# A mixture-of-experts block on one core: one table load before the expert loop, the second half's transposes one unit earlier, relu and silu back to back

## The reference

```python
def expert_block(args):
    xb, e = args
    gu = xb @ w_gate_up[e] + b_gate_up[e]
    gate = jnp.minimum(gu[:, :D_FF], SWIGLU_LIMIT)
    up = jnp.clip(gu[:, D_FF:], -SWIGLU_LIMIT, SWIGLU_LIMIT)
    act = (up + 1.0) * (gate * jax.nn.sigmoid(SWIGLU_ALPHA * gate))
    return act @ w_down[e] + b_down[e]
```

## Time and profile before

| | us |
|---|---|
| median of 3 runs | 2231.53 (2229.44 to 2234.69) |
| profiled execution, its own time | 2228.01 |
| its span, first to last instruction | 2226.2 |
| PE busy | 2065.4 (93%) |
| expert loop, first `turn_rows` to last `down` | 741 to 2185 |

### The profile page before, as it was taken

One profiled execution on the slowest core, in us unless ns is written; L12 is line 12 of the kernel. 1 busy time (PEld: TensorE's weight loads), 2 busy tenths in 40 slices (PEclk: granted clock), 3 DMA queues, 4 the chain that ended last, 5 costly groups with the idle time before them and its releaser, 6 DMA issues.

```text
span 2226.2 us, 37885 instructions
## 1 busy us (share of the span) xinstructions
PE 2065.4 (93%) x11367; PEld 1602.5 (72%) x11368; DVE 1540.9 (69%) x1941; ACT 1467.8 (66%) x1944; POOL 397.0 (18%) x519
## 2 busy tenths in 40 slices
PE   6889999899886599999999999999999999999997
PEld 4678778777675478787787777777776777676683
DVE  4466565544456678889798687886785787675595
ACT  4466676643331478888787686786785787675583
POOL 2222212011234111111121121111110111011022
PEclk9899999869797799999999999999999999999996
DMA  5301010211115699999799898998996899796694
GB/s 177 62 21 29 20 29 20 76 48 57 40 59 182 235 308 371 379 369 378 274 363 326 285 337 287 320 371 276 312 377 225 296 343 314 276 315 242 219 318 177
DMA packets 250411, 507.21 MB, mean 228 GB/s; under 512 B 44454, under 2 KB 62676, under 8 KB 250228
## 3 DMA queue, kind: packets, MB, share of 16 engines
q1 hardware_dynamic: 234724, 462.98, 59.0%
q0 software_dynamic: 15632, 43.53, 7.6%
HBM read 470.25 MB, written 38.54 MB: 229 GB/s over the span
## 4 chain that ended last, share of the span: by engine, by line
PE 68%; DVE 12%; issue 10%; ACT 5%; DMA 4%; POOL 1%; DVEq 0%; SPq 0%; ACTq 0%; POOLq 0%
PE bank L1038 23%; PE bank L1060 12%; PE bank L1072 6%; PE bank L809 6%; DVE w_low L1858 6%; PE bank L908 4%; PE bank L1089 3%; PE bank L890 2%; PE bank L837 2%; PE bank L852 2%; DMA rel_rows<-rel_row 2%; PE bank L879 2%; PE bank L1154 1%; PE bank L1028 1%; DVE act_low L1872 1%
## 5 line engine op out<-in xcount | busy, mean ns | idle before, releaser
L1858 DVE TENSOR_TENSOR w_low<-gu_w,w_high 128x1024 fp32r<-128x1024 f32 x528 | 619.7, 1221 | 241.6 <-ACT w_high L1397 233.7
L1397 ACT CAST w_high<-gu_w 128x1024 fp32r<-128x1024 f32 x528 | 534.7, 1050 | 162.6 <-PE bank L1038 86.5
L1038 PE MATMUL bank<-w_high,x_high 128*128 128x512 f32 x1056 | 415.8, 394 | 3.1 <-DVE w_low L1858 3.1
L1038 PE MATMUL bank<-w_high,x_low 128*128 128x512 f32 x1056 | 413.4, 392 | 0.0
L1038 PE MATMUL bank<-w_low,x_high 128*128 128x512 f32 x1056 | 413.0, 391 | 0.0
L1858 DVE TENSOR_TENSOR w_low<-dn_w,w_high 128x1024 fp32r<-128x1024 f32 x264 | 315.0, 1224 | 19.7 <-ACT w_high L1397 13.3
L1397 ACT CAST w_high<-dn_w 128x1024 fp32r<-128x1024 f32 x264 | 270.9, 1050 | 23.2 <-PE bank L1038 13.1
L1060 PE MATMUL bank<-w_high,act_high 128*128 128x512 f32 x528 | 212.5, 403 | 23.7 <-DVE act_low L1872 23.7
L1038 PEld LDWEIGHTS bank<-w_high,x_high 128*128 128x128 f32 x1056 | 198.8, 188 | 46.4 <-DVE w_low L1858 3.8
L1038 PEld LDWEIGHTS bank<-w_high,x_low 128*128 128x128 f32 x1056 | 198.7, 188 | 42.6
L1038 PEld LDWEIGHTS bank<-w_low,x_high 128*128 128x128 f32 x1056 | 198.9, 188 | 41.9
(11 more groups left out here) (233 smaller groups left out, 3221.2 us busy)
## 6 DMA issues: line engine op xcount, KB each, us to landing
gu_w<-in_w_gate_up SPq DMA_DIRECT2D x528, 512.0 KB, 11.3
dn_w<-in_w_down SPq DMA_DIRECT2D x132, 1024.0 KB, 18.4
w_st<-in_w_in SPq DMA_DIRECT2D x14, 512.0 KB, 3.9
xt<-in_x SPq DMA_DIRECT2D x8, 512.0 KB, 3.6
wo_sb<-in_w_out SPq DMA_DIRECT2D x2, 2048.0 KB, 7.5
x<-in_x SPq DMA_DIRECT2D x8, 512.0 KB, 4.2
residual_rows<-x SPq DMA_DIRECT2D x8, 512.0 KB, 2.6
h_rows<-h SPq DMA_DIRECT2D x8, 512.0 KB, 2.9
```

The lines of the kernel that those rows point to most:

```text
L1038: mm = pe.matmul(bank[:, 2 * h + g, :], a[:, k, :], b, start=False, stop=last)
L1397: act.copy(w_high[:, u % RING, :], src).then_inc(high_ready, 1)
L1858: dve.tensor_tensor(w_low[:, u % RING, :], raw, w_high[:, u % RING, :], ALU.subtract).then_inc(split_ready, 1)
```

## The change

A load of table set 18 is written ahead of the loop on ACT; in the built program it takes the place of both loads in the loop. On PE the transposes of half 1 move ahead of the fourth down unit. On ACT and DVE the Silu and the product follow relu and clamp directly, with the one unit's cast or subtraction that stood between them now behind; the cast and the low part of half 1's activations move ahead of unit 23's.

```diff
-                down(i, range(4))
+                down(i, range(3))
                 turn_hidden(i, 1)
+                down(i, range(3, 4))
                 by_class(n_tok, lambda parts: turn_over(i, parts))
...
+            load_tables(SILU_TABLES)
             act.wait_ge(d_bias, 32)
...
                 room(i, 0)
-                high_part(i, range(12, 13))
                 silu(i, 0)
-                high_part(i, range(13, 17))
+                high_part(i, range(12, 17))
                 act_high_part(i, 0)
                 high_part(i, range(17, 20))
                 room(i, 1)
+                silu(i, 1)
                 high_part(i, range(20, 21))
-                silu(i, 1)
                 over_silu(i, n_tok)
-                high_part(i, range(21, 24))
+                high_part(i, range(21, 23))
                 act_high_part(i, 1)
+                high_part(i, range(23, 24))
                 over_turned(i, n_tok)
...
                 clamp(0)
-                low_part(range(12, 13))
                 hidden_out(0)
-                low_part(range(13, 17))
+                low_part(range(12, 17))
                 act_low_part(0)
                 low_part(range(17, 20))
                 clamp(1)
+                hidden_out(1)
                 low_part(range(20, 21))
-                hidden_out(1)
...
-                low_part(range(21, 24))
+                low_part(range(21, 23))
                 act_low_part(1)
+                low_part(range(23, 24))
                 x_low_part(i + 1)
```

More of the change, by code:

```diff
@@ L37 @@
 LIMIT, ALPHA = 7.0, 1.702
-LN_EXP_TABLES = 6
+LN_EXP_TABLES, SILU_TABLES = 6, 18
 QK_CHUNKS, V_CHUNKS = 13, 5
@@ L1168, in chain, with load_tables @@
                 act.wait_ge(act_step, steps[0])
-            act.add_instruction(mybir.InstLoadActFuncSet(
-                name=nc.get_next_instruction_name(), act_func_set_id=LN_EXP_TABLES,
-                engine=mybir.EngineType.Activation, ins=[], outs=[]))
+            def load_tables(number):
+                act.add_instruction(mybir.InstLoadActFuncSet(
+                    name=nc.get_next_instruction_name(), act_func_set_id=number,
+                    engine=mybir.EngineType.Activation, ins=[], outs=[]))
+            load_tables(LN_EXP_TABLES)
             def square(t):
```

## The result

| | before | changed |
|---|---|---|
| median, us | 2232.07 (4 runs, 2229.44 to 2234.69) | 2200.9 (4 runs, 2198.03 to 2202.37) |
| ratio, 95% interval | | 0.987 (0.9853 to 0.9887) |
| the same kernel once more (e9 below) | 2225.72 (11 runs, 2218.45 to 2236.51) | 2205.05 (6 runs), 0.9898 (0.9867 to 0.9928) |
| span of the profiled execution | 2226.2 | 2197.8 |

The account below looks back on a forecast made before the run. PE, busy 93%, was bound in the loop by waits for `act_low`, late through DVE's queue and late transposes. Gaps 22.6, start 1.0, gathers -1.6 give 22.0 us: median 2231.5 to 2209.5 us, range 2204 to 2219.

Parts of the forecast that it names:

- The gaps: PE's waits for `act_low` in 28 of 33 items, 23.7 us; closing them was to give 22.6 us.
- walk through DVE's queue: Half 1's steps on DVE timed in the new order: `act_low` done at 1016.7, PE may start at 1016.8.
- brackets: Most each item's closed gap could give PE: 1.46 us in the item walked through, 0.17 to 0.39 with own extras.
- 23.7, less 11 x 0.1: All gaps for `act_low` close, except 0.1 us left in each of 11 items without extras here and next: 22.6 us.
- The start: Item 0, where the removed table load delays the first casts: up to 1.3 us, taken as 1.0 for the clock.
- The gathers: In seven successive items without extras, SP cannot follow PE, so PE waits about 1.6 us for gathered rows.
- PE's lead to 7.8 us against a slack of 6.2: By the gather issued at 1039.58, six items' closed gaps put PE 7.8 us ahead; its rows had 6.2 to spare.
- slower: Rival: the gather comes late everywhere, 6 us in each of 19 items, about 2269 us; chance 0.03.
- no difference: Rival: another step replaces `act_low` as last to arrive, or transposes between matmuls cost more; about 2229 us; chance 0.05.
- DVE staying late: Rival: removing the load gives DVE nothing in half 1, 0.45 us stays in 11 items; 2212.3 us; chance 0.17.
- SP's lag binds: Rival: transfers, 36.64 us an item on SP, bind in every item without extras; 2217.0 us; chance 0.13.
- units 12 or 20: Sign of a wrong forecast: a PE wait for `w_low` at these units; unit 12 was given two us of cover.

Follow-up runs that it names:

- e9: The changed kernel measured again with no edit; median 2205.1 us, ratio to before 0.9898.
- e3: Changed kernel with each item's slot loads issued ahead of the previous item's down weights' refill instead of behind it; median 2197.3 us, ratio to before 0.9854.
- e5: Changed kernel with half 0 on ACT and DVE back in the order of before; median 2198.5 us, ratio to before 0.9877.
- e2: Changed kernel without the load ahead of the loop, so both table loads stand in the loop again; median 2209.7 us, ratio to before 0.9912.
- e8: Changed kernel with early slot loads plus 22 unused matmuls on constants before PE's wait for the first gather; median 2195.2 us, ratio to before 0.9865.

## Why the prediction missed

The mechanism was right point by point; the size was not, and the range was too narrow. The medians of the first comparison fell by 31.2 us where 22.0 were forecast. Of the 9.2 us between them 2.8 lie in the loop, 3.6 before and behind it, and 2.8 in how the medians lie to the profiled executions. Working against the first pair of traces, 28.4 us of span against 22.0 forecast:

* *The gaps (22.6 forecast).* All 28 closed, as the prediction's walk through DVE's queue had it. Even the order of ends held: `act_low` is last by 0.02 us in the walk (1016.8 against 1016.78) and by 0.15 in the trace. But the gaps are worth more than their brackets: items 1 to 31 had 22.0 us of them and gained 24.2 in e3. With item 0 (0.6) and item 32 (1.3) the term is 26.1. **The mis-sized step is "23.7, less 11 x 0.1".** Nearly all of the surplus is in the eight items with extras of their own, which had 2.7 us of gaps and gained 4.7. The ten without extras here and next had 13.7 and gained 14.0, so the 0.1 us left in each was not there; the eight where only the next has extras had 5.7 and gained that. The brackets count from the modelled end of the transposes, 1.04 us behind the start of the eight, while PE in the changed kernel starts the next matmul 0.79 us behind it in items with extras of their own and 0.94 in those without.
* *The start (1.0 forecast).* Bias matmul to first hidden matmul went from 4.27 to 2.56 us. Item 0 shrank by 3.1 in all, 2.4 of it besides its gap; in e9 and e5 by 2.4 and 1.8 in all. The load's own share is as read from the rows: ACT's first cast of the loop starts 3.55 us behind the start of its last `xo` copy before, and 2.28 behind it in the changed kernel, 1.27 less. The other part goes with the clock, which rose 5.7 us after the bias matmul in the changed kernel's profile and 9.0 before. Over the changed kernel, e3 and e5 to e9 item 0 takes 51.6 us where the clock rises after 5.7 us, 52.1 to 52.4 where it rises after 6.2 to 7.2, and 52.8 to 52.9 where it rises after 7.7 to 7.8. So the 2.4 are in part luck.
* *The gathers (-1.6 forecast).* The place, the items and SP's 36.64 us an item were right; the wait was -3.8. **The step that fell short is the one that set PE's lead to 7.8 us against a slack of 6.2.** Counted from the first bias matmul, PE's lead at the last of these rows, had it not waited, is 11.6 us: 8.5 from the six items instead of 7.8, and 3.1 from item 0, which the sum left out. The gather came 2.3 us earlier too (its landing went from 300.97 to 298.62 us behind that matmul), so the slack was 8.5, and the difference is the three waits of 1.0. The wait of the extras' own gather (0.69), which lands behind the first, was not counted.
* *The rest.* 3.2 us lie before the loop, where only the load was added, in ACT's idle time before the gather, and 0.4 behind it. e9 had the part before the loop 4.6 us later than before instead of 3.2 earlier, and so only 19.6 us less of span.

The loop from first bias to last down matmul thus gained 24.8 us in the first profile and 24.1 in e9, against 22.0. **The range failed** because it took the scatter as 2.5 us from three runs; sets of 11, 14 and 17 further runs of before span 2218.5 to 2236.5. The first comparison's 31.2 us fell outside, the second's 21 (22.7 by the ratio) would have been inside. The second agreement is in part luck: the loop gained 24.1 in e9, too. The rivals: slower and no difference are out by both intervals; DVE staying late is out (e2 has its 0.39 to 0.48 us, but only with the loads left in); SP's lag binds, but only where seven items without extras follow each other, and through the slot loads' place (e3); the gathers still land in 7.1 to 7.7 us there; neither units 12 or 20 nor a drain of the table load made a wait.

## What to carry to other kernels

Follow the queue of the engine whose result comes last, not the busiest engine: 84.6 us of table loads were worth 6.5 us in items 1 to 31, and the new order, with one subtraction moved behind `act_low` and four transposes moved one unit forward, 19.0. When a gap of some 1.4 us in each turn of a loop is closed, look at once for what ran at nearly the same pace beside it (here SP, 36.64 against 37.2 us an item), and which of its deliveries has the least slack. And before a range is drawn, ask how far runs of one kernel scatter; compare parts of the trace that don't hold the scatter.

## What was not expected of the hardware

The granted clock differs between executions of one kernel before the loop (first transposes at 737.6 and 745.7 us in the two profiles of the changed kernel) and not within it (1.00 from item 0's first units to its end). And a stretch of PE work that had brought the clock to 1.00 did not keep it there in e8: it fell to 0.5 behind gaps of 1.6 and 0.7 us, and stayed there for 10 us, over two further gaps of 2.0 and 1.5. What the chip looks at when it decides so these runs don't show.
